# Expert weights in 17 landing places instead of 15, and the read-back rows in used places

## What is computed

```python
global_i = g_idx[:, None] * EXPERTS_PER_GROUP + top_i          # two experts of 32 for each token
combine = jnp.sum(one_hot(global_i, N_EXPERTS) * top_w[..., None], axis=1)
for e in range(N_EXPERTS):
    hid = jax.nn.silu(t @ w_gate[e]) * (t @ w_up[e])           # 1024 -> 512, twice
    out = out + combine[:, e:e + 1] * (hid @ w_down[e])        # 512 -> 1024
```

## Time and profile before

| | |
|---|---|
| median of 3 runs | 1885.23 us (1883.31 to 1886.85) |
| the profiled execution's own time | 1886.12 us |
| its span, first to last instruction | 1884.3 us |
| TensorE busy | 1739.5 us (92%) |
| VectorE busy | 1003.0 us (53%) |
| ScalarE busy | 637.1 us (34%) |
| GpSimd busy | 95.1 us (5%) |
| mean granted TensorE clock | 0.972 |
| read from HBM | 387.74 MB |

### The profile page before, as it was taken

One profiled execution on the slowest core, in us unless ns is written; L12 is line 12 of the kernel. 1 busy time (PEld: TensorE's weight loads), 2 busy tenths in 40 slices (PEclk: granted clock), 3 DMA queues, 4 the chain that ended last, 5 costly groups with the idle time before them and its releaser, 6 DMA issues.

```text
span 1884.3 us, 22342 instructions
## 1 busy us (share of the span) xinstructions
PE 1739.5 (92%) x8421; PEld 1141.7 (61%) x8421; DVE 1003.0 (53%) x1762; ACT 637.1 (34%) x1142; POOL 95.1 (5%) x100
## 2 busy tenths in 40 slices
PE   7999999999999989999999998889697978988887
PEld 6887777777788867777775544555353433433322
DVE  5988655555678875545675797643522122222113
ACT  5544555444455445544443211220111101111111
POOL 1000000000000000000000320100001001000001
PEclk9999999999999999999999999899898999999999
DMA  7544434345565454343555442323199899999998
GB/s 246 165 149 133 144 115 127 110 126 165 149 185 173 119 159 124 113 135 107 154 180 169 141 134 87 104 89 112 69 379 365 344 418 419 421 419 419 421 421 327
DMA packets 131465, 392.63 MB, mean 208 GB/s; under 512 B 15532, under 2 KB 17344, under 8 KB 106784
## 3 DMA queue, kind: packets, MB, share of 16 engines
q1 hardware_dynamic: 126752, 386.65, 58.2%
q0 software_dynamic: 4608, 4.56, 0.8%
HBM read 387.74 MB, written 10.17 MB: 211 GB/s over the span
## 4 chain that ended last, share of the span: by engine, by line
PE 64%; DVE 15%; DMA 14%; ACT 4%; issue 3%; SPq 0%; POOL 0%; DVEq 0%; ACTq 0%; POOLq 0%
PE bank L696 10%; PE bank L698 10%; PE bank L697 10%; PE bank L747 9%; PE bank L1145 7%; DMA r<-in_w_up 5%; PE bank L1162 5%; DMA r<-in_w_gate 4%; DMA spare<-in_w_up 3%; DVE w_lo L1252 2%; DVE r L1252 2%; DVE r L1258 2%; PE bank L823 2%; PE bank L664 2%; DMA w_raw<-in_w_up 1%
## 5 line engine op out<-in xcount | busy, mean ns | idle before, releaser
L1252 DVE TENSOR_TENSOR w_lo<-w_raw,w_hi 128x1024 fp32r<-128x1024 f32 x266 | 320.5, 1216 | 224.4 <-ACT w_hi L2240 223.6
L696 PE MATMUL bank<-w_hi,h_hi 128*128 128x512 f32 x800 | 327.6, 409 | 13.4 <-DVE w_lo L1252 13.4
L2240 ACT CAST w_hi<-w_raw 128x1024 fp32r<-128x1024 f32 x266 | 277.4, 1047 | 164.4 <-PE bank L698 157.2
L698 PE MATMUL bank<-w_hi,h_lo 128*128 128x512 f32 x800 | 315.6, 394 | 0.0
L697 PE MATMUL bank<-w_lo,h_hi 128*128 128x512 f32 x800 | 315.3, 394 | 0.0
L696 PEld LDWEIGHTS bank<-w_hi,h_hi 128*128 128x128 f32 x800 | 152.3, 190 | 50.1 <-issue 14.3
L698 PEld LDWEIGHTS bank<-w_hi,h_lo 128*128 128x128 f32 x800 | 152.3, 190 | 34.0
L697 PEld LDWEIGHTS bank<-w_lo,h_hi 128*128 128x128 f32 x800 | 152.9, 191 | 29.1
L1145 PE MATMUL bank<-r,window 128*64 128x512 f32 (+2 forms) x424 | 118.9, 621 | 27.0 <-DMA r<-in_w_gate 24.0
L747 PE MATMUL bank<-w_raw,h_all 128*128 128x512 f32 (+1 forms) x320 | 142.3, 601 | 1.1 <-DVE h_all L1252 1.1
L2411 ACT ACTIVATE r<-bank,small 128x256 f32<-128x256 f32 (+1 forms) x152 | 63.8, 425 | 206.5 <-DVE small L1255 206.5
(11 more groups left out here) (352 smaller groups left out, 2439.7 us busy)
## 6 DMA issues: line engine op xcount, KB each, us to landing
w_raw<-in_w_in SPq DMA_DIRECT2D x236, 512.0 KB, 3.7
w_raw<-in_w_proj SPq DMA_DIRECT2D x48, 512.0 KB, 3.7
r<-in_w_gate SPq DMA_DIRECT2D x20, 1024.0 KB, 22.2
r<-in_w_up SPq DMA_DIRECT2D x20, 1024.0 KB, 24.0
spare<-in_w_gate SPq DMA_DIRECT2D x19, 1024.0 KB, 25.8
spare<-in_w_up SPq DMA_DIRECT2D x18, 1024.0 KB, 20.3
spare<-in_w_down SPq DMA_DIRECT2D x14, 1024.0 KB, 26.7
w_raw<-in_w_down SPq DMA_DIRECT2D x14, 1024.0 KB, 27.5
```

The lines of the kernel that those rows point to most:

```text
L696: e.matmul(out_, sh, mh, start=first, stop=False, skip_group_check=shared)
L698: return e.matmul(out_, sl, mh, start=False, stop=last, skip_group_check=shared)
L1252: o.did(v.tensor_tensor(out_, a, b, op), sem, value)
L2240: a.copy(halves(n)[0], raw_of(n)).then_inc(w_hi, 1)
```

## The change

The ring gets two more places, R[6] and R[3], 17 in all. Since R[3] holds the low half of `ht` until the tokens are selected, SyncE waits before load 16, the first one into R[3], for the last of the selection's groups on TensorE. The rows read back at the end go into the places of the last two loads whose block's rows are stored before the gathers (loads 178 and 179). The zeros come from a part of `scratch[3]` that nothing else uses, 128x128, which the DMA reads four times to write the same 64 rows in pieces of 512 bytes.

```diff
-        in_moe = [sem(f"in_moe{i}") for i in range(15)]
+        in_moe = [sem(f"in_moe{i}") for i in range(17)]
...
         PLACES = ([R[i][:, :] for i in range(7, 11)] + [spare[i][:, :] for i in (1, 2, 3, 5, 4)] + [w_raw[:, i * 2 * D:(i + 1) * 2 * D] for i in range(3)]
-                  + [spare[0][:, :], y_flat[:, :], h_flat[:, :]])
+                  + [spare[0][:, :], y_flat[:, :], h_flat[:, :], R[6][:, :], R[3][:, :]])
...
-        own_rows = [[R[i][:, 0:D], R[i][:, D:2 * D]] for i in (3, 6)]
+        last_scattered = 6 * (EXP - 2)
+        own_rows = [[PLACES[q % len(PLACES)][:, 0:D], PLACES[q % len(PLACES)][:, D:2 * D]] for q in (last_scattered - 2, last_scattered - 1)]
+        zeros = scratch[3][:, 3 * P:4 * P]
...
                         g.wait_ge(scattered[0], 16)
-                        o.did(g.memset(own_rows[0][0][0:P // 2, :], 0.0))
+                        o.did(g.memset(zeros, 0.0))
                         o.prev()
-                        g.dma_start(d["y_rows"][LAST_START[-1]:SLOTS, :], own_rows[0][0][0:P // 2, :]).then_inc(rows_cleared, 16)
+                        g.dma_start(d["y_rows"][LAST_START[-1]:SLOTS, :].rearrange("r (a f c) -> (r a) f c", a=2, f=4), zeros.unsqueeze(1).to_broadcast([P, 4, P])).then_inc(rows_cleared, 16)
                         g.wait_ge(rows_cleared, 16)
...
                         if q >= len(PLACES):
                             s.wait_ge(m_used, last_use[q - len(PLACES)] + 1)
+                        if q == len(PLACES) - 1:
+                            b, k = acc[("xs", SLOT_QUARTERS - 1, 3)]
+                            s.wait_ge(full[b], k)
                         s.dma_start(PLACES[q % len(PLACES)], source[:, j * 2 * D:(j + 1) * 2 * D]).then_inc(in_moe[q % len(PLACES)], 16)
```

## The result

| | before | after |
|---|---|---|
| median (5 runs each) | 1885.23 us (1883.31 to 1886.85) | 1877.34 us (1872.82 to 1878.48) |
| ratio, 95% interval | | 0.9941 (0.9928 to 0.9955) |
| span of the profiled execution | 1884.3 us | 1875.9 us |
| first expert load issued at | 1359.33 us | 1361.41 us |
| from there to the end ("the stage") | 525.0 us | 514.5 us |

The forecast was 1875.2 us, in a range of 1872.0 to 1880.5. The median of these five runs is 7.9 us lower than before; the comparison of the runs gives 0.59%, or 11 us, and the stage itself lost 10.5 us. The profiled execution came to the stage 2.1 us later than the one before, which hides as much of the gain.

What follows compares the result with a forecast made beforehand. The stream of expert loads, dry in two gaps, was taken as the bound. Four loads' time, 4 x 2.50 = 10.0 us, with all other parts at cost 0, gave 1885.23 - 10.0 = 1875.2 us, range 1872.0 to 1880.5.

Steps and rivals of the forecast that it cites:

- The bound: Expert stage: it ends when the stream of 192 loads ends plus a tail; after 1510 no idle DMA time to win.
- First gap, 5.0 us: Idle DMA time from 1405: two more loads go before it, 8.8 us shrinks to 3.8, later loads land 5.0 us earlier.
- Second gap, another 5.0: Idle DMA time from 1495: 7.8 us shrinks to 2.8, so what follows is 10.0 us earlier in all.
- rival B: Second gap closes because shorter waits keep TensorE's clock up: gain 12.5 us, 1872.7 us; chance 0.08.
- The price of a load: Expert loads of 1 MiB at 420 GB/s: 2.50 us each, four loads' time 10.0 us.
- The new wait: SyncE before load 16 waits for TensorE's last selection group, already over when SyncE gets there at about 1378: cost 0.
- the zeros: GpSimd's write in 512-byte pieces takes 4 us, under a 7.2 us cover: cost 0, between 0 and 0.5 us of stream time.
- the rows read back: Four gathers at the end land in places of loads 178 and 179, where no load comes after: cost 0.
- A: Only the first gap counts, TensorE does not reach load 30 five microseconds earlier: gain 5.0 us, 1880.2 us; chance 0.11.
- D: Loads are not let out, SyncE held before load 16 or places busy longer: nothing changes, 1885.2 us; chance 0.05.
- C: Loads into R[3] and R[6] slow the stream: 3.2% less rate makes it 3.8 us slower, 1889 us; chance 0.03.
- no wait for a load near 1855.3: End of the stage: TensorE's last wait on a load was expected near 1855.3, with the same 19 us behind it.

Runs made afterwards that it cites:

- 16 places: The change with only R[6] added to the ring, not R[3], and no wait for the selection: 1880.4 us, 0.9973 against before.
- 13 places: The kernel before with the ring's two last tiles left out: 1902.0 us, ratio 1.0077.
- 15 places by release: The kernel before, but each load takes the place that falls free first instead of a fixed order: 1874.5 us, 0.9923.
- loads held to 1402: The change, but SyncE holds loads 15 and 16 until TensorE has left load 3: 1877.7 us, 0.9955 against the kernel before.
- 16 places by release: Ring with R[6] but not R[3], each load taking the place that falls free first: 1869.7 us, 0.9911 against the kernel before.
- 17 places by release: The change, but each load takes the place that falls free first: 1867.9 us, again 1869.3 us; 0.9910 and 0.9911 against the kernel before.
- the change's second profile: The changed kernel measured once more, nothing altered: 1874.9 us, 0.9949 against the kernel before.
- 15 places and the rest: The change without its two more places and without SyncE's wait for the selection: 1886.8 us, 1.0014 against the kernel before.
- loads held to 1391: The change, but SyncE holds loads 15 and 16 until the first release of a place: 1875.0 us, 0.9938 against the kernel before.

## Why the prediction held

- **The bound.** The stage is set by the stream of loads, and only idle DMA time ahead of 1510 could be won. Shown: the change of the stage follows the change of the lost time: 16 places -5.4 and -5.4, the change -10.5 and -10.9, 13 places +14.4 and +14.2 with the third stretch, 15 places by release -13.8 and -14.2, loads held to 1402 -8.6 and -8.7. The two part by more with 16 places by release, -16.7 and -17.8, and with 17, -17.8 and -19.5. Some of that lies at the end: with the change and with 17 places by release, the part behind the last expert's gate matrix is 0.3 us longer than before. The rest, over 1 us with 17 by release, is not explained.
- **First gap, 5.0 us.** Measured 4.9 by bytes (10.9 to 6.0), and load 30 came 5.1 us earlier. TensorE could follow, as its 10.1 us of idle time said.
- **Second gap, another 5.0.** Measured 6.0 by bytes (8.8 to 2.8), and 10.7 us at the end of the wait behind it. The release that ends this gap came 6.0 us earlier, not 5.0: 5.1 from the end of the wait for load 30, and the eight matmuls behind it took 5.37 us against 6.14 before, so 0.8 us of rival B is in it. That is not a steady effect: the same group took 5.22 us in the change's second profile, but 6.26 in both the kernel with loads held to 1391 and the one with 15 places and the rest, which wait as long. With loads held to 1391 the release was as early as with the change only because the wait for load 30 had ended 6.2 us earlier, not 5.1.
- **What was left.** The sizes of the two gaps were too small: 8.8 and 7.8 us by the DMA share, 10.9 and 8.8 us by the bytes. This did not hurt the sum, which was made of loads and not of gaps. It did hurt what was expected of release order with 17 places: 5.9 us under the change, where 7.3 were measured.
- **The price of a load.** Four loads' time came to 10.5 us in the stage, 2.6 us each, and to 2.7 us each with 16 places. The saturated stretches moved 419 to 420 GB/s, which is 2.50 us. The half microsecond over 10.0 is the 1.0 us that the second gap gave beyond its two loads, less 0.3 to 0.4 us at the end of the stage. By the 358 GB/s of the Trainium skill (DMA: Bandwidth & Descriptors, "Where 436 GB/s comes from") the estimate would have been 11.7 us; the trace's rate does not agree with it on this one core, though the sum lies between the two.
- **The new wait, the zeros, the rows read back: 0.** Shown by the kernel with everything but the places (525.0 us) and the one held to 1391 (514.5). The price taken for the zeros' write, 4 us, was 3.0 and 3.9 in the two profiles of the change, but up to 7.8 where loads ran beside it, over the cover of 7.2; the term stayed at nothing because the stage has no loss from it, not because of the bounds.
- **The signs.** Loads 15 and 16 went out at 1378.12 and 1380.30, load 21 at 1419.66, which is 1417.6 and the 2.1 us of the later start, and the share from 1405 to 1425 was 0.79 for 0.81. One sign failed: no wait for a load near 1855.3 (1857.4 with the later start) with 19 us behind it. The last expert's gate matmuls took 3.21 us instead of 1.94, and its up matrix was then there in time; the last wait for a load ended at 1848.87, with 27.0 us behind it. The total hardly moved, as the same part was 26.7 us before.
- **Two slips.** The text says that four stretches of the earlier trace rows stand at a share of 1.00 or 1.01; they are three. It says that half of the stretch from 1434 runs at the lower clock; an average of 0.82 between full and half clock is 36% of it. No number hangs on either.
- **Rivals.** A and D fell by the runs with 16 and 17 places, C by 419 to 420 GB/s in the saturated stretches. B was there in part, as said.
- **1875.2 against 1877.3.** In the profiled execution the difference lies ahead of the stage. By the stage alone the span would have been 1884.3 - 10.5 = 1873.8 us; it was 1875.9, since the stage began 2.1 us later. The second set of runs gave 1874.9. That both medians came so near to 1875.2 is in part chance, as single executions of one kernel lie several microseconds apart; the stage is the firmer proof.

## What to carry to other kernels

When a stream of transfers is the bound later on, find where it runs dry earlier and ask which buffer's release the next load waits for; here two buffers more were worth about two transfers' time for each dry stretch (4.9 and 6.0 us), and in no stretch can they win more than its size. Before adding buffers, look at whether others are already free when the queue waits for the next one in a fixed order: here taking the first that falls free gave more with 15 places than 17 gave in fixed order, and both together 17.8 us. Judge a change to one stage by that stage's own length in the profile, when the part ahead of it scatters by more than the gain.

## What the runs showed of the hardware

- A DMA share read as "busy" understates what a dry stretch costs. Between 1395 and 1430 of the kernel before the share is 0.75, so 8.8 us idle, but 289 GB/s of 420 is 10.9 us; over both stretches 16.1 by the share and 19.7 by the bytes. The clearest case is the ring of 13, whose stage grew by 14.4 us: 14.2 by the bytes, 11.0 by the share. For the change itself the two measures, 10.9 and 10.5, can't be told apart by the stage, and for 17 places by release the stage (17.8) lies between them.
- The time ahead of the experts, with the same code, lay between 1354.91 and 1366.13 us in twelve profiles. Between the two extremes TensorE's busy time for the same 5,993 matmuls differs by 11.3 us and its idle time by 0.1. With a stage that repeats within 0.1 us (514.5 and 514.4; 507.2 and 507.3) that is nearly all of the scatter.
- A write of 256 KB to HBM from GpSimd in 512 pieces of 512 bytes landed in 2.8 and 3.0 us in a dry stretch, no slower than the 3.0 us of the same bytes from rows of 4 KB, and in 7.2 to 7.8 us beside streaming loads, where rows of 4 KB took 7.4 us.
